# Order of the expert weight loads on SP's queue: down weights behind their own gate and up, in a streaming-encoder block with a mixture of experts

## What is computed

```python
def moe_ffn(h, w_router, router_bias, we_gate, we_up, we_down, ws_gate, ws_up, ws_down):
    scores = jax.nn.sigmoid(jnp.dot(t, w_router))
    ...
    gates = ...          # 8 experts of 64 for each token, their weights
    out = (jax.nn.silu(t @ ws_gate) * (t @ ws_up)) @ ws_down
    for e in range(N_EXPERTS):
        hid = jax.nn.silu(t @ we_gate[e]) * (t @ we_up[e])
        out = out + gates[:, e:e + 1] * (hid @ we_down[e])
    return out.reshape(b, s, d)
```

## Time and profile before

| | us |
|---|---|
| median of 3 runs | 684.05 |
| lowest, highest | 682.99, 684.23 |
| the profiled execution's own time | 683.22 |
| its span, first to last instruction | 681.5 |
| PE busy | 621.6 (91%) |
| DVE busy | 257.5 (38%) |
| ACT busy | 123.5 (18%) |
| POOL busy | 39.9 (6%) |
| moved by DMA | 250.75 MB, mean 368 GB/s |

### The profile page before, as it was taken

How to read it: one execution, slowest core, us unless ns; L and a number is a source line. 1 busy time by engine, 2 the same in 40 slices (tenths; PEclk the granted TensorE clock), 3 DMA queues, 4 the chain that set the end, 5 groups by cost and what they waited for, 6 DMA issues and landing times.

```text
span 681.5 us, 11730 instructions
## 1 busy us (share of the span) xinstructions
PE 621.6 (91%) x4454; PEld 345.0 (51%) x4454; DVE 257.5 (38%) x706; ACT 123.5 (18%) x267; POOL 39.9 (6%) x223
## 2 busy tenths in 40 slices
PE   2589999998999999999999999979999999999892
PEld 0278887844554454545353545533355445544440
DVE  0129948777663323233223232231133132332115
ACT  2320313211611111111111111111111111111112
POOL 8000000000012000101000000000000001000000
PEclk9789999999999999999999999989999999999996
DMA  8996895465489999999999999999999999999951
GB/s 341 384 401 261 333 394 194 189 256 233 186 347 421 422 418 421 421 420 419 421 421 420 418 420 421 420 421 421 420 420 420 420 421 420 421 421 420 419 208 64
DMA packets 39868, 250.75 MB, mean 368 GB/s; under 512 B 4657, under 2 KB 6785, under 8 KB 11777
## 3 DMA queue, kind: packets, MB, share of 16 engines
q1 hardware_dynamic: 38256, 248.56, 88.9%
q10 hardware_dynamic: 1554, 1.41, 0.6%
HBM read 248.91 MB, written 1.05 MB: 367 GB/s over the span
## 4 chain that ended last, share of the span: by engine, by line
PE 72%; DMA 15%; DVE 8%; ACT 2%; issue 1%; SPq 1%; ACTq 0%; DVEq 0%
PE PS L1391 12%; PE PS L1600 11%; PE PS L1596 10%; DMA ring<-in_we_up_dram 10%; PE PS L1575 8%; PE PS L1637 5%; PE PS L1606 5%; DMA ring<-in_w_in_dram 5%; PE PS L1632 4%; PE PS L1659 3%; PE PS L1655 2%; PE PS L1642 2%; PE PS L1521 2%; DVE MOD L883 2%; PE PS L1615 1%; DVE YLO L1210 1%
## 5 line engine op out<-in xcount | busy, mean ns | idle before, releaser
L1391 PE MATMUL PS<-hT,ring 128*128 128x256 f32 x384 | 86.6, 385 | 3.9 <-DMA ring<-in_w_in_dram 3.9
L1600 PE MATMUL PS<-ring,arena 128*64 128x256 f32 x736 | 88.4, 391 | 0.3 <-DMA ring<-in_we_up_dram 0.3
L1391 PEld LDWEIGHTS PS<-hT,ring 128*128 128x128 f32 x384 | 73.6, 193 | 15.4 <-issue 5.5
L1199 DVE SCALAR_TENSOR_TENSOR arena<-arena,gate,PS 128x128 f32<-128x128 f32 (+1 forms) x44 | 16.6, 378 | 168.4 <-ACT arena L808 168.3
L1210 DVE TENSOR_TENSOR YLO<-PS,YHI 128x512 fp32r<-128x512 f32 x54 | 37.2, 689 | 97.0 <-ACT YHI L819 97.0
L1596 PE MATMUL PS<-ring,arena 128*32 128x512 f32 x576 | 69.4, 633 | 3.8 <-DMA ring<-in_we_up_dram 3.8
L1575 PE MATMUL PS<-G,H2HI 128*128 128x256 f32 (+1 forms) x240 | 62.9, 298 | 8.0 <-ACT arena L799 7.0
L1600 PEld LDWEIGHTS PS<-ring,arena 128*64 128x64 f32 x736 | 50.2, 134 | 32.6 <-issue 4.1
L819 ACT CAST YHI<-PS 128x512 fp32r<-128x512 f32 x54 | 31.7, 586 | 162.9 <-PE PS L1637 80.6
L1575 PE MATMUL PS<-G,H2LO 128*128 128x256 f32 (+1 forms) x240 | 58.4, 278 | 0.0
L1575 PEld LDWEIGHTS PS<-G,H2HI 128*128 128x128 f32 x240 | 45.5, 190 | 20.6 <-issue 9.9
(11 more groups left out here) (263 smaller groups left out, 599.4 us busy)
## 6 DMA issues: line engine op xcount, KB each, us to landing
ring<-in_we_gate_dram SPq DMA_DIRECT2D x64, 1024.0 KB, 16.7
ring<-in_we_up_dram SPq DMA_DIRECT2D x64, 1024.0 KB, 19.4
ring<-in_we_down_dram SPq DMA_DIRECT2D x64, 1024.0 KB, 16.9
ring<-in_w_ada_dram SPq DMA_DIRECT2D x6, 3072.0 KB, 15.5
ring<-in_w_in_dram SPq DMA_DIRECT2D x3, 3072.0 KB, 15.8
ring<-in_w_ada_dram SPq DMA_DIRECT2D x3, 2048.0 KB, 7.3
ring<-in_w_out_dram SPq DMA_DIRECT2D x1, 3072.0 KB, 19.6
ring<-in_w_in_dram SPq DMA_DIRECT2D x1, 1568.0 KB, 27.4
```

Source lines behind the costliest of these rows:

```text
L1391: mm = pe.matmul(PS[:, 2 + q % QB, 0:TOK], w[:, k, (m % 6) * P:(m % 6) * P + P], hT[:, k, :], start=(k == 0), stop=(k == KD - 1))
L1600: m = pe.matmul(PS[64 * c:64 * c + 64, 6, 0:FE].rearrange("p (a n) -> p a n", a=2), xt[:, k, :], gu_cols(w[0], k, c), start=(k == 0), stop ...
```

## The change

The down weights of a load are issued directly behind its own gate and up, with the wait that belongs to them, and no longer behind the gate and up of the load that follows. Which wait belongs to which transfer, the slots, and the work of all other engines stay as they are.

```diff
             sp.wait_ge(order_ready, 1)
-            before = None
-            for q in range(FIXED, NE):
+            which = {}
+
+            def next_gate_up(q):
                 s = SLOT[q]
-                e = expert(q)
+                which[q] = expert(q)
                 if q >= NSLOT:
                     sp.wait_ge(gu_done, POS_OF[PROC[q - NSLOT]] + 1)
...
-                load_gate_up(s, we_gate[0, e], we_up[0, e], gu_loaded[s])
-                if before is not None:
-                    if q - 1 >= NSLOT:
-                        sp.wait_ge(down_ps, parts_before(POS_OF[PROC[q - 1 - NSLOT]] + 1))
-                    elif SLOT[q - 1] == slot_of(load_no(S, 0)):
-                        sp.wait_ge(sy_ps, 2 * TT)
-                    load_down(SLOT[q - 1], we_down[0, before], down_loaded[SLOT[q - 1]])
-                before = e
-            sp.wait_ge(down_ps, parts_before(POS_OF[PROC[NE - 1 - NSLOT]] + 1))
-            load_down(SLOT[NE - 1], we_down[0, before], down_loaded[SLOT[NE - 1]])
+                load_gate_up(s, we_gate[0, which[q]], we_up[0, which[q]], gu_loaded[s])
+
+            def next_down(q):
+                s = SLOT[q]
+                if q >= NSLOT:
+                    sp.wait_ge(down_ps, parts_before(POS_OF[PROC[q - NSLOT]] + 1))
+                elif s == slot_of(load_no(S, 0)):
+                    sp.wait_ge(sy_ps, 2 * TT)
+                load_down(s, we_down[0, which[q]], down_loaded[s])
+
+            for q in range(FIXED, NE):
+                next_gate_up(q)
+                next_down(q)
```

## The result

The changed kernel takes **702.68 us** (median of 4 runs, 698.50 to 707.84) against 683.67 us before (682.99 to 684.23): the ratio is **1.0279**, with a 95% interval of 1.0248 to 1.0310. That is 19.0 us slower; the forecast was 10.2 us slower, 694.3, with a range up to 699.5. The sign and the place were right, the size was not. Note the spread too: four runs of before lie within 1.3 us, four of after within 9.3.

What follows compares the result with a forecast made beforehand. The prediction took the transfer stream, through PE's last wait for up(62), as the bound. Place 2.5 plus queue shortages 7.7 gave 10.2 us later, on the 684.05 median 694.3 us; range 686.0 to 699.5.

Steps and rivals of the forecast that it cites:

- The bound: Expert stretch: the transfer stream decides, through PE's last wait for up weights, up(62), at gate_up of position 42.
- a sign of being wrong: In the profile after, down weights appearing among PE's releasers would show the prediction wrong.
- The place term: At PE's last wait, up(62) moves one place later in the transfer queue: +2.5 us.
- Where the queue is short: Losses at down(4), (5), (8), (23), (41), (44); all other down loads in time, down(7), (20), (26) by 1 to 2 us.
- The size of a shortage: At six down loads, landing is the later of previous landing +2.5 and issue +4.8; losses sum to 7.7 us.
- cheaper restarts: Bound at the short-queue places: if restarts are wholly hidden, only down(4) costs, 1.2 us; +3.7 us in all.
- Rival B, the clock: Positions 0, 2, 4: late PE loses clock and releases slots later, three 1.6 us steps; +15.0 us, 699.1; chance 0.15.
- Rival A: Whole stretch: the queue holds and only up(62)'s place counts; +2.5 us, 686.6; chance 0.13.
- C: Transfer stream: a shorter queue lets the slowest DMA ring keep up; -2.3 us, 681.8; chance 0.04.
- D: Transfer stream: half of the shorter queue's gain, 2.4 us, cancels the 2.5 us place cost; no change, 684; chance 0.06.
- The tail: From the start of gate_up of position 42, near 657, to the end: as long as before, about 34 us.
- By the Trainium skill: At the six restarts, the page's 4.4 us estimate makes each 0.4 us cheaper, the forecast up to 2.4 us earlier.

Runs made afterwards that it cites:

- the second profile: The changed kernel run once more, unaltered, against before: 702.73 us, ratio 1.0287; its profiled execution took 704.2 us.
- the sixth run: Changed order from load 4 on, loads 2 and 3 in the order of before, so up(3) keeps its place: 701.63 us, ratio 1.0263 to before.
- the seventh: The whole change plus ten additional 128x128 matmuls on PE ahead of gate_up of positions 0 and 4: 703.33 us, ratio 1.0307 to before.
- the third: Changed order for loads 2 to 8 only, the order of before from there on: 692.99 us, ratio 1.0142 to before.
- run four: Against before, each down goes behind the gate and up of the load two further on: 682.07 us, ratio 0.9973.
- run five: Order of before for loads 2 to 8, changed order from load 9 on: 693.9 us, ratio 1.0176 to before.

## Why the prediction was wrong, point by point

**The bound: right.** The stream of transfers decides, by the landing of up(62). One swapped transfer at load 61 moved the time by 3.3 us, and 47 reordered loads by the same. Down weights appear nowhere among PE's releasers in the profile of after, which would have been a sign of being wrong.

**The place term: 2.5, measured 3.3** (two runs), with 0.6 of the rest, in the first of them, in the longer gate_up behind a longer wait, which the prediction had left out.

**Where the queue is short: right.** Restarts or near-restarts came at down(4), (5), (8), (23), (41) and (44), as forecast, gate_up of position 0 started at 204.1 (forecast near 204), and gate(5) at 216.45 (near 215). Beyond these, down(7), (20) and (50) came short; the first two the working had in time by 1 to 2 us, and all other down loads in time.

**The size of a shortage: wrong. This is the step that failed.** The prediction took a landing as the later of the landing before plus 2.5 and the issue plus 4.8, and so priced the six shortages at 7.7 us. Along the profile of after the shift ran away from the forecast like this (the second profile in brackets):

| place | forecast, us | measured, us |
|---|---|---|
| 9, down(4) | 3.5 | 4.9 (4.8) |
| 21, down(8) | 5.2 | 10.3 (7.9) |
| 66, down(23) | 5.6 | 14.4 (12.3) |
| 129, down(44) | 7.7 | 18.9 (15.3) |
| up(62), without its 2.5 for the place | 7.7 | 19.6 (18.1) |

Adding the two kinds of delay over all transfers issued less than 5 us ahead of the last landing: by the rule 11.2 us (9.2), and beyond the rule **10.9 us (8.9)**. They add up to 22.1 us (18.1), against a shift of 19.6 (18.1) at up(62); late landings behind a full queue, which before has too, make up the difference. The second kind was put at zero. The rows of before hardly show it: at the start of its stretch gate(3) was issued 2.65 us ahead of the last landing and came 0.4 us late, and down(5), 4.86 ahead, 0.4 us late, and from there on no transfer was issued less than 5 us ahead; the prediction said so ("No row shows a queue that empties in mid-stream"), and bounded the term by cheaper restarts on one side, and on the other only by PE's clock. It should have been bounded by a dearer one. The first kind grew as well, from the forecast's 7.7 to 11.2, since each late landing makes PE late and with it the next release: down(8) was issued at 248.14, forecast 245.4, and down(20), in time by 1 to 2 us in the forecast, was issued 0.3 us behind the last landing and cost 2.6 us.

**Rival B, the clock.** It happened at two of its three places: 2.93 us of waiting and 5.43 us for gate_up of position 0, and again at position 4; at position 2 the wait was 1.81 us and the clock stayed up. Its 699.1 was nearer to the measured 702.7 than the forecast was, but by luck: with the clock held up at both places, the time stayed (1.0307 against 1.0279, the intervals overlap). So it isn't the cause of the missing 9 us. Later falls feed back as well, as at down(41) in the sixth run; in the seventh the mean granted clock is as high as before's, and 18 us are lost all the same.

**Rival A, C, D.** A is what 47 of the 62 loads do. C and D asked for a shallower queue to run faster, and nothing of the kind showed: the median step is 2.48 us in before and in both profiles of after. The 2.511 that the prediction read as the pace is a mean that holds a few long steps.

**The tail: nearly right.** Forecast as long as before, 34 us; measured 36.3, as position 43 waits 1.89 us for up(63) and runs at the lower clock. Position 42 waited 2.40 us, forecast 3 to 4, and started at 669.8, forecast near 657.

**By the Trainium skill,** "DMA: Bandwidth & Descriptors", section "Anatomy of one DMA", a restart would have been 0.4 us cheaper. The page gives that fit for transfers that GpSimd issues, which the prediction left out; these are issued by SP. The run that met an empty queue on purpose has 4.6 to 4.9 us for seven of eight single transfers, so that the measured 4.8 was the one to take.

## What to carry to other kernels

When a queue of transfers is what bounds a kernel, ask of each reordering two things: does the transfer that the consumer waits for move back (here that cost 3.3 us at the last wait: one transfer time of 2.5, and the rest in part in the longer gate_up), and does any wait now hold the queue while less than some 5 us is left in it. Keep the transfers whose slots come free late behind those whose slots come free early; here one more step in that direction even gained 0.3%. A forecast that hangs on a margin of 1 to 2 us at a dozen places should take its range from all of them going wrong, not from the listed six.

## What the runs showed of the hardware that was not expected

A full queue has a median step of 2.48 us per 1024 KB before, but it isn't regular to the end: the 178 steps from place 8 to 186 took 447.0 us, 4.8 us more than that, most of it in a few steps of 3.1 to 3.8 us with 15 us and more queued. A single transfer on an empty queue takes 4.6 to 4.9 us in seven cases of eight. Between the two, with 2 to 4 us left, a transfer lands up to 2.8 us later than either would have it, in about half the cases and not in the same ones from run to run. The two profiles of after differ by it, and by what each late landing does to the next release; that the whole spread of 9 us comes from there isn't shown.

The length of a single wait of PE doesn't tell whether the granted clock falls. It fell to half behind waits of 0.7 and 0.8 us only (490 to 498 us in the sixth run, and at the same work in the third), behind 1.89 us at position 43 of after, and behind 2.93 and 3.12 us there. It stayed up behind 2.40 us at position 42 of after, 2.68 and 3.04 us in run four, and 3.17 us in run five.
